# Seven modulation ticks in place of five per row tile pair, and the first feed-forward's gate summed inside that feed-forward

## The reference, cut to what matters

```python
for l in range(2):
    mod = silu(c) @ w_mod[l] + b_mod[l]                  # 1024 x 9216
    sh1, sc1, g1, sh2, sc2, g2, sh3, sc3, g3 = split(mod, 9)
    h = rmsnorm(x) * (1 + sc1) + sh1
    x = x + 0.5 * g1 * ((silu(h @ w_gate1[l]) * (h @ w_up1[l])) @ w_down1[l])
    h = rmsnorm(x) * (1 + sc2) + sh2
    x = x + g2 * mixer(h, ...)
    h = rmsnorm(x) * (1 + sc3) + sh3
    x = x + 0.5 * g3 * ((silu(h @ w_gate2[l]) * (h @ w_up2[l])) @ w_down2[l])
```

## Time and profile before

| | |
|---|---|
| device time, median of 3 runs | 1557.58 us (1552.69 to 1558.09) |
| the profiled execution | 1557.58 us, span 1555.8 us |
| TensorE matmul busy | 1467.1 us (94%) |
| TensorE weight load busy | 1127.3 us (72%) |
| VectorE busy | 1017.0 us (65%) |
| ScalarE busy | 697.0 us (45%) |
| GpSimd busy | 301.0 us (19%) |
| mean share of the granted TensorE clock | 0.974 |
| HBM read | 304.11 MB, 196 GB/s over the span |
| chain that ended last, by engine | PE 79%, DVE 11%, ACT 6%, POOL 2% |

### The profile page before, as it was taken

The page is one execution under the profiler, slowest core; times in us unless marked ns, Lnnn a source line. Parts: engine busy times, 40 slices in busy tenths (PEclk is TensorE's granted clock), DMA queues, the critical chain, the costliest instruction groups (busy, mean ns, idle before and its releaser), DMA issues.

```text
span 1555.8 us, 18934 instructions
## 1 busy us (share of the span) xinstructions
PE 1467.1 (94%) x7424; PEld 1127.3 (72%) x7424; DVE 1017.0 (65%) x1531; ACT 697.0 (45%) x1115; POOL 301.0 (19%) x269
## 2 busy tenths in 40 slices
PE   6998999989799999999989999899999999999998
PEld 4557457446688887875678878788887865688887
DVE  3476876635488886454678885688874563786654
ACT  4435230424366543541455653465532631466552
POOL 0424092005101110151411110111100341311100
PEclk9998989979999999999999999899999999999999
DMA  9544443331578887332358987479895422477551
GB/s 384 197 135 136 149 177 104 127 123 54 162 251 294 295 341 267 110 107 86 115 195 279 314 309 273 139 267 318 292 341 168 134 69 100 143 237 256 188 191 55
DMA packets 159641, 306.41 MB, mean 197 GB/s; under 512 B 5952, under 2 KB 115776, under 8 KB 148672
## 3 DMA queue, kind: packets, MB, share of 16 engines
q1 hardware_dynamic: 159120, 304.93, 56.7%
q10 hardware_dynamic: 432, 0.27, 0.1%
HBM read 304.11 MB, written 1.08 MB: 196 GB/s over the span
## 4 chain that ended last, share of the span: by engine, by line
PE 79%; DVE 11%; ACT 6%; POOL 2%; issue 1%; DMA 0%; SPq 0%; DVEq 0%; ACTq 0%; POOLq 0%
PE ps L445 78%; PE ps L448 1%; DVE H L1927 1%; DVE arena L1293 1%; DVE arena L1290 1%; ACT arena L1557 1%; DVE ring L555 1%; DMA X<-in_x_dram 0%; DVE H L1876 0%; DVE misc L1590 0%; DVE arena L2741 0%; DVE arena L1279 0%; POOL arena L2480 0%; DVE H L1861 0%; DVE wlo L2103 0%
## 5 line engine op out<-in xcount | busy, mean ns | idle before, releaser
L445 PE MATMUL ps<-hh,whi 128*128 128x512 f32 x1408 | 491.4, 401 | 5.8 <-DVE hh L2109 5.8
L2103 DVE TENSOR_TENSOR wlo<-ring,whi 128x1024 fp32r<-128x1024 f32 x264 | 321.1, 1227 | 162.4 <-ACT whi L2042 160.0
L2042 ACT ACTIVATE whi<-ring 128x1024 fp32r<-128x1024 f32 x264 | 274.5, 1055 | 243.7 <-PE ps L445 241.0
L445 PE MATMUL ps<-hh,wlo 128*128 128x256 f32 x1408 | 367.2, 281 | 0.0
L445 PEld LDWEIGHTS ps<-hh,whi 128*128 128x128 f32 x1408 | 255.1, 189 | 60.7 <-DVE hh L2109 6.7
L445 PEld LDWEIGHTS ps<-hh,wlo 128*128 128x128 f32 x1408 | 267.3, 190 | 16.0
L445 PE MATMUL ps<-ring,H 128*128 128x512 f32 (+1 forms) x544 | 235.2, 583 | 10.6 <-ACT arena L2243 5.6
L445 PEld LDWEIGHTS ps<-ring,H 128*128 128x128 f32 x544 | 101.2, 193 | 118.3 <-issue 102.8
L555 DVE SCALAR_TENSOR_TENSOR ring<-ring,cb 128x1024 f32<-128x1024 f32 x144 | 178.8, 1243 | 4.4 <-DMA ring<-in_mods_dram 4.1
L2092 POOL TENSOR_TENSOR alo<-H,ahi 128x256 fp32r<-128x256 f32 x88 | 70.5, 802 | 466.7 <-ACT ahi L2080 463.2
L445 PE MATMUL ps<-H,ring 128*128 128x256 f32 (+1 forms) x576 | 155.5, 428 | 1.2 <-DVE arena L2255 0.6
(11 more groups left out here) (343 smaller groups left out, 1549.2 us busy)
## 6 DMA issues: line engine op xcount, KB each, us to landing
ring<-in_mods_dram SPq DMA_DIRECT2D x76, 1024.0 KB, 5.6
ring<-in_w_in_dram SPq DMA_DIRECT2D x48, 1024.0 KB, 5.2
ring<-in_ffn_w_gate_dram SPq DMA_DIRECT2D x44, 1024.0 KB, 5.5
ring<-in_ffn_w_up_dram SPq DMA_DIRECT2D x44, 1024.0 KB, 7.0
ring<-in_ffn_w_down_dram SPq DMA_DIRECT2D x44, 1024.0 KB, 5.2
ring<-in_w_out_dram SPq DMA_DIRECT2D x12, 1024.0 KB, 5.0
ring<-in_w_first_dram SPq DMA_DIRECT2D x8, 1024.0 KB, 12.6
gates<-gate_rows SPq DMA_DIRECT2D x7, 512.0 KB, 5.8
```

The lines of the kernel that those rows point to most:

```text
L445: return self.e.matmul(o, lhsT, rhs, start=start, stop=stop)
L2042: a.done(a.e.activation(hi, M.slot(key)[:, r0:r0 + rn, :], ACT.Copy), ("whi", l, sub, n))
L2103: v.done(v.e.tensor_tensor(lo, M.slot(key)[:, r0:r0 + rn, :], plain(hi), ALU.subtract), ("split", l, sub, n), *([M.freed(key)] if ends els ...
```

## The change

Two lines. Part 3, the gate of the first feed-forward, leaves the list "first" and heads the list of the first feed-forward, (0, 0), which then has six parts (96 ticks) in place of five (80); "first" has three parts (48 ticks) in place of four (64). The lists of the other three feed-forwards keep their parts: four, five and one. And `beside` gives 2, 1, 2, 2 ticks for the four quarters of a pair in place of 1, 1, 1, 2, in all four feed-forwards, for VectorE and for SP's fetches alike: 77 ticks over the 11 pairs in place of 55. The total of modulation work is the same.

```diff
@@ -506,7 +506,7 @@
-    M.mods = {"first": made[0:4], (0, 0): made[4:9], (0, 2): made[9:13], (1, 0): made[13:18], (1, 2): made[18:19]}
+    M.mods = {"first": made[0:3], (0, 0): made[3:9], (0, 2): made[9:13], (1, 0): made[13:18], (1, 2): made[18:19]}
@@ -2002,7 +2002,7 @@
 def beside(f, q):
 
-    return 2 if q == 3 else 1
+    return 1 if q == 1 else 2
```

## The result

| | device time, median | ratio to before |
|---|---|---|
| before, run beside it | 1555.59 us (1552.69 to 1558.09, 4 runs) | |
| after | 1583.36 us (1582.19 to 1584.16, 4 runs) | 1.0174 [1.0151, 1.0197] |

A forecast was written before the change was run, and what follows sets the result against it. With the change VectorE's in-order loop, not TensorE's 11.27 us a pair, was taken to bound gate and up. 9.0 + 5.1 + 8.5 + 0.1 + 0 - 2.0 = +20.7 us on 1557.58 gave 1578.3 us, range 1569 to 1588.

The forecast's parts named there:

- The loop: Gate and up pairs: VectorE's in-order loop takes T(k) = 3.62 + (4 + k) x 1.14 us for k modulation products.
- T(3): VectorE's loop from one pair's first sum to the next with three modulation products: 11.6 us.
- T(4): VectorE's loop from one pair's first sum to the next with four modulation products: 12.74 us.
- the weight loads' wait: First feed-forward: TensorE's weight loads' wait for sums L2124 should rise from 1.5 to about 8 us.
- Rival A: Gate and up pairs: VectorE's idle time takes the added products and no pair grows; 1552.4 us, chance 0.07.
- SP's own waits are priced at nothing: SP's waits and added fetches cost nothing, as five ring slots cover them; bound +6, 1 us for each of six gates.
- The sign that was named: In the feed-forwards: VectorE waiting for modulation tiles would show the forecast wrong; late tiles were priced at +6 us.
- The third part: Layer 0's third part, gate and up: ninth sum +6.8 us, down products starting at 928.8 against 923.74, +5.1 us.
- The attention: The attention loses the gate's eight products and gains 2.0 us; bounds nothing and 3.5 us.
- Rival C: Attention: a wait of 5.6 us could let TensorE return to 2.4 GHz sooner; down to 1570 us, chance 0.10.
- Rival B: Inside the pairs: 12 new stalls of 1.5 us pull TensorE's clock down, 0.5 us each; 1584 us, chance 0.15.
- The down products: Losing ticks saves nothing; start gaps give +1.6 us in the first feed-forward, -1.6 in the third part, sum 0.

The follow-up runs named there:

- six_ticks: The changed kernel with six ticks a pair (1, 1, 2, 2), three products in every pair; 1573.13 us, 1.0078 against before.
- eight_banks: The changed kernel with eight PSUM banks in place of six for gate and up; 1588.69 us, 1.0172 against before.
- filled_idle: The changed kernel with VectorE's ticks of quarter 3 moved ahead of that quarter's low part; 1580.27 us, 1.0120 against before.
- down_order: The changed kernel with SyncE fetching the first down weights in order of use, among the last pair's modulation tiles; 1579.04 us, 1.0150 against before.
- ticks_only: The kernel before with seven ticks a pair alone, the gate left in the first block; 1588.84 us, 1.0175 against before.
- gate_only: The kernel before with the gate's move alone, five ticks a pair kept; 1560.39 us, 1.0020 against before.
- last_free: The kernel before with no ticks beside the last pair before its sum, two behind it, gate not moved; 1553.18 us, 0.9972 against before.
- gate_along: The kernel before with the gate moved, five ticks a pair, and two or three ticks per down product step; 1557.05 us, 0.9997 against before.

## Why the prediction was right, and where its sizes were off

**The loop.** This step held in each part. T(3) measured 11.62, T(4) with L559 12.96, the 1.44 us of idle time stayed in each loop, the weight loads' wait rose to 10.0 us (8 were forecast), and `six_ticks` and `eight_banks` moved as the formula has it. Rival A, that the steps fit into the idle time, is refuted by the sums' distances. `filled_idle` shows that even a product moved into that time gains 0.1 to 0.5 us a loop and not 1.14.

**The term that was mis-sized.** "SP's own waits are priced at nothing": the added tiles delay the first down weights behind them in SyncE's order. It cost 5.2 us in the last loop of the first feed-forward (17.92 for 12.74) and 2.2 in that of layer 1 (14.97), and `down_order` took both back. Together that is 7.4 us, above the bound of +6. That bound was put on six gates at 1 us, and the price fell on the two feed-forwards whose ticks reach the last pair. The sign that was named, VectorE waiting for modulation tiles, hardly shows: 5.0 us in the whole execution, for 4.1 before. It was a weight tile that came late.

**Terms that were off the other way.** The first sum came 12.19 us behind TensorE's start in place of 13.7 in both these feed-forwards, as TensorE's clock did not fall there: busy time by stretch over the first 14 us, before and after:

```profile
428.40:442.40 14.00, 14.00 (x71) 12.12 (x72) 10.30 (x12) 7.80 (x11) 0.00 (x0) 0.88 0.67 217
```

```profile
426.10:440.00 13.90, 13.89 (x78) 11.88 (x79) 12.36 (x15) 9.23 (x13) 0.00 (x0) 1.00 0.78 258
```

That gave back 1.5 and 1.9 us. The first feed-forward is then 9.0 + 5.3 - 1.5 = +12.8, and that of layer 1 8.5 + 2.4 - 1.9 = +9.0.

This gain can't be called the change's. In the traces of all fourteen kernels the first sum comes either 12.1 to 12.2 or 13.6 to 14.1 us behind the start of its feed-forward, and both values occur with either edit: `ticks_only` has 13.68 and 13.69 in these two stages, `down_order` 13.68 and 12.13. In the trace of before two of the four stages are late, in that of after none, in that of `eight_banks` all. So 3.4 us of the closeness of the forecast to the profiled execution are luck. What decides between the two values is open; no run was made for it.

**The third part** came to +6.3 for +5.1. Its ninth sum stands 110.3 us behind the start (forecast 110.2), so the 1.1 that are left lie behind it: the down products start 23.5 us after that sum, and 22.4 were forecast. The forecast took the 1.63 us from copy to down products from the last feed-forward, where they start 0.74 us behind the pair's first sum. In the third part they start 0.74 us behind its second sum, at 942.31:

```profile
941.57 0.69 DVE L2124 TENSOR_TENSOR H<-H,ps 128x512 f32<-128x512 f32 x1 [0.47 <-ACT H L2073]
```

That sum is 1.15 us behind the first (940.42), which is the difference.

**The attention** gave more than the 2.0 us forecast and its bound of 3.5. From its start to the first feed-forward it took 153.91 us before and 153.88 in `ticks_only`, but 150.15 in the changed kernel and 149.57 in `gate_only`: 3.8 and 4.3 us. The wait forecast at 5.6 us accounts for 1.1 of them. The rest, priced at 0.9, was too low by 1.8 or more, and which products it lies behind was not traced. In the profile of after 1.5 us of it is hidden, as the attention started that much later (275.96 for 274.49). That is not shown to come from the change: `last_free`, which leaves the gate, starts it at 276.57. Rival C did not come: TensorE ran at 0.51 for 15.4 us after the wait of 5.64.

**The clock.** Rival B's stalls inside the pairs did not pull it down: 0.99 over the stage. The down products went as forecast in size, +1.7 in the first and -1.6 in the third part. The waits ahead of them did not: 7.78 us and not 2.6 for the first, 1.41 and not 0.5 for the third part. The first figure held even so, as a wait of 2.70 us in `down_order` was also followed by 61.70.

The sum: 20.7 forecast, 25.0 in the span; 1578.3 forecast, 1582.63 in the profiled execution.

## What to carry to other kernels

Before work is added to an engine's idle time, ask where in its queue that time stands. In an in-order loop over several engines the idle time behind a wait can't be used by what stands behind the same wait, and the engine is the bound at 84% busy. Work placed ahead of the instruction that frees another engine's resource, above all the last one before a stage changes, can cost its full duration. Here the last sum came 1.15 us sooner in each of three stages when one product was moved behind it, TensorE's wait shrank by 0.6 to 1.15 us, and the kernel got faster.

A step that brings its own transfers also moves every fetch behind it in the shared ring. Look at the first fetch of the next stage.

## What the runs showed of the hardware that was not expected

- A two-input operation of GpSimd (128x256) took 0.74 us while VectorE waited and 1.65 us while it worked. The two low parts of VectorE beside it took 3.06 us in place of 2.35. With GpSimd writing zeros in its place (0.31 us) VectorE's low parts were at their old duration.
- In the traces kept, waits of TensorE of 0.25 to 1.53 us ahead of down products that no fetch and no leftover held up were followed by 60.10 to 60.19 us for them, and waits of 2.33 us and more by 61.6 to 62.8. In between it goes both ways. Two waits of 2.0 us in `gate_along` (TensorE's timeline) went apart: the first was followed by 61.74 us at a granted clock of 0.97, the second by 60.12 at 1.00. What decided there is open.

```profile
930.12 0.73 PE L445 MATMUL ps<-whi,ahi 128*128 128x512 f32 x1 [2.00 <-DVE H L2124]
...
1129.59 0.47 PE L445 MATMUL ps<-whi,ahi 128*128 128x512 f32 x1 [2.04 <-DVE H L2124]
```

- The fetch of one down tile took 9.85 us to its landing beside the others, where the median of its kind in that execution is 5.2.
